# A decoder step on one core: other orders at the stage boundaries

## The reference

```python
x += W_out [ dilated sliding-window attention(q,k,v) || conformer convolution(glu) ],  [q|k|v|glu] = RMSNorm(x) @ W_in
x += PEER(RMSNorm(x));   y = RMSNorm_final(x)

# PEER: 8 heads, 128 x 128 product keys, top 16 of the candidates, 16384 experts
q = x @ w_query                      # per head two halves of 128
s1, s2 = q1 @ k1.T, q2 @ k2.T        # top 16 of each, sums, top 16 of the sums -> eid, softmax -> gate
act = gelu(sum(exp_u[eid] * x))      # one dot product per chosen expert
out = sum(gate * act * exp_v[eid])
```

## Time and profile before

| | |
|---|---|
| median of three runs | 1831.47 us |
| the profiled execution | 1835.39 us, of which span 1833.6 us |
| TensorE busy | 1738.1 us (95%) |
| VectorE busy | 1430.8 us (78%) |
| ScalarE busy | 620.0 us (34%) |
| GpSimd busy | 442.8 us (24%) |
| chain that ended last | TensorE 60%, VectorE 16%, ScalarE 3%, DMA 2% |
| granted TensorE clock, mean | 0.982 of full speed |
| moved by DMA | 397 MB, 216 GB/s |

### The profile page before, as it was taken

One profiled execution on the slowest core, in us unless ns is written; L12 is line 12 of the kernel. 1 busy time (PEld: TensorE's weight loads), 2 busy tenths in 40 slices (PEclk: granted clock), 3 DMA queues, 4 the chain that ended last, 5 costly groups with the idle time before them and its releaser, 6 DMA issues.

```text
span 1833.6 us, 26115 instructions
## 1 busy us (share of the span) xinstructions
PE 1738.1 (95%) x9365; PEld 1523.3 (83%) x9365; DVE 1430.8 (78%) x3029; ACT 620.0 (34%) x1022; POOL 442.8 (24%) x510
## 2 busy tenths in 40 slices
PE   7998889899999899979999999999999999989986
PEld 6777664477676478879999999999999999988885
DVE  5887552279999788857888888887888888878887
ACT  5223451211111177643333333333333333322322
POOL 1000000013232200023444444433333333332210
PEclk9999999899999999989999999999999999999998
DMA  8314603222211257688889889888888889877763
GB/s 264 112 65 169 248 1 110 96 70 70 80 47 57 70 157 218 210 286 291 290 306 325 296 308 332 296 299 299 289 309 317 305 308 318 313 256 265 259 217 132
DMA packets 200148, 396.97 MB, mean 216 GB/s; under 512 B 14863, under 2 KB 132653, under 8 KB 198605
## 3 DMA queue, kind: packets, MB, share of 16 engines
q1 hardware_dynamic: 158549, 244.29, 39.2%
q0 software_dynamic: 41472, 151.01, 23.4%
HBM read 359.55 MB, written 34.29 MB: 215 GB/s over the span
## 4 chain that ended last, share of the span: by engine, by line
PE 60%; DVE 16%; issue 3%; ACT 3%; DMA 2%; POOL 0%; SPq 0%; DVEq 0%; ACTq 0%
PE bank L1496 23%; PE bank L1436 23%; PE bank L1470 5%; PE bank L1418 4%; PE bank L1357 3%; PE bank L1395 2%; DVE ef L1900 1%; DVE catT_then_yT L2054 1%; DVE y L2075 1%; DVE sc L1825 1%; DVE i L1822 1%; DVE i L1831 1%; DVE y0s L2075 1%; ACT u_high L1636 1%; DVE bits L1863 1%
## 5 line engine op out<-in xcount | busy, mean ns | idle before, releaser
L1496 PE MATMUL bank<-p_high,v_high 128*128 128x400 f32 x880 | 304.1, 346 | 7.5 <-DVE v_low L2000 7.5
L1496 PE MATMUL bank<-p_high,v_low 128*128 128x400 f32 x880 | 305.1, 347 | 0.0
L1496 PE MATMUL bank<-p_low,v_high 128*128 128x400 f32 x880 | 304.8, 346 | 0.0
L1436 PE MATMUL bank<-h_high,u_high 128*128 128x400 f32 x768 | 264.3, 344 | 10.6 <-DVE u_low L2000 9.9
L1436 PE MATMUL bank<-h_high,u_low 128*128 128x400 f32 x768 | 266.7, 347 | 0.0
L1436 PE MATMUL bank<-h_low,u_high 128*128 128x400 f32 x768 | 264.9, 346 | 0.0
L1735 POOL DMA_INDIRECT rows<-in_u_rows,row_u x144 | 194.2, 1349 | 279.4 <-DVE dots L2066 242.7
L1735 POOL DMA_INDIRECT rows<-in_v,row_u x144 | 162.6, 1129 | 351.5 <-DVE y L2075 283.6
L1642 ACT CAST p_high<-gel 128x400 fp32r<-128x400 f32 x128 | 67.4, 527 | 375.3 <-DVE gel L2045 373.7
L2000 DVE TENSOR_TENSOR v_low<-vv,v_high 128x1024 fp32r<-128x1024 f32 x110 | 134.7, 1225 | 65.6 <-ACT v_high L1636 65.5
L1418 PE MATMUL bank<-h2T,early 128*128 128x400 f32 x512 | 179.2, 505 | 5.5 <-ACT gel L1583 5.5
(11 more groups left out here) (254 smaller groups left out, 2962.3 us busy)
## 6 DMA issues: line engine op xcount, KB each, us to landing
vv<-in_v SPq DMA_DIRECT2D x110, 512.0 KB, 7.2
u<-in_uT SPq DMA_DIRECT2D x96, 512.0 KB, 4.8
gates_kept<-staged SPq DMA_DIRECT2D x10, 2560.0 KB, 10.0
gate<-gates_kept SPq DMA_DIRECT2D x30, 800.0 KB, 7.4
early<-in_uT SPq DMA_DIRECT2D x32, 512.0 KB, 3.4
w_in_sb<-in_w_in SPq DMA_DIRECT2D x9, 1024.0 KB, 8.1
u<-in_v SPq DMA_DIRECT2D x18, 512.0 KB, 6.4
wq<-in_w_q SPq DMA_DIRECT2D x16, 512.0 KB, 3.5
```

Of the source, the lines that this page charges most:

```text
L1436: ins = pe.matmul(a_ps[par][:, 0:DT], x[:, par, k], y, start=(z == 0), stop=(z == len(order) - 1))
L1496: ins = pe.matmul(out, x[:, c, at:at + P], y, start=(opens and c == 0 and n == 0), stop=(closes and c == CG - 1 and n == 2))
```

## The change

It has nine edits, all of order, apart from the halved squares.
1. The first query product (head 0, half 0, z 0) is made ahead of the turn of tile 4; it waits for the first three tiles of h2T and for `joined`.
2. Eleven early activations behind head 7 in place of ten (`IN_HEADS`), so two behind the slots and eight among the gates; seven gelus ahead of the exponential.
3. The eight casts of h_high move into blocks 1 to 8 of the gates; `hot` of batch 0 is cast ahead of the last gelu.
4. In group 23 the last chunk of u is multiplied at the end of the group.
5. In groups 24 to 31 the steps m and p come as m m p p, and the piece that the group needs in product 4 comes first.
6. SyncE loads piece 2 ahead of piece 1 in group 24, and waits for one product of u fewer for it.
7. x_back and gf are loaded ahead of the transfers of group 31.
8. The product with `joins` stands behind product 2 instead of 3.
9. Squares at the end by halves, each half as soon as it is summed, the root with the first half as its bias; the sums, scales and gains in another order.

```diff
-IN_HEADS = {0: 1, 1: 2, 2: 2, 3: 2, 4: 2, 5: 2, 6: 2, 7: 10}
+IN_HEADS = {0: 1, 1: 2, 2: 2, 3: 2, 4: 2, 5: 2, 6: 2, 7: 11}
...
+    if last:
+        heavy.append(heavy.pop(heavy.index(("a", CG - 1))))
     if wide:
         heavy = [("w", x[1] + 1) if x[0] == "w" else x for x in heavy]
+        products = [(x, c) for c in range(0, CG, 2) for x in "mmpp"]
+        wanted = [x for x in heavy if x[0] not in "mp"]
+        heavy = wanted[:1] + [(x, c + n % 2) for n, (x, c) in enumerate(products[:4])] + wanted[1:4] + [
+            (x, c + n % 2) for n, (x, c) in enumerate(products[4:])] + wanted[4:]
         if not entered:
-            heavy.insert([x[0] for x in heavy].index("w"), ("w", 1))
+            heavy = heavy[1:5] + [("w", 1)] + heavy[:1] + heavy[5:]
...
                 if wide(part, gg) and m >= 2:
-                    sp.wait_ge(a_done, NK)
+                    sp.wait_ge(a_done, NK - 3 + m)
...
             def group(part, gg):
+                if (part, gg) == (PARTS - 1, GROUPS - 1):
+                    load_back()
...
-                    if what == "w":
+                    if what == "w" and GROUPS * part + gg == WIDE + 1 and at[0] in (1, 2):
+                        load_v(*of_group(part, gg, 3 - at[0]))
+                    elif what == "w":
                         load_v(*of_group(part, gg, *at))
...
                     out_projection(i)
+                if i == TILES:
+                    pe.wait_ge(h_taken, 2 * (HT // P + 1))
+                    pe.wait_ge(joined, 1)
+                    query(0, 0, 0)
                 if i:
                     turn(i - 1)
...
-                    if q == EARLY - IN_GATES - 1:
+                    if q == EARLY - IN_GATES - 2:
                         turn_slots()
...
-                if m == 3:
+                if m == 2:
                     pe.wait_ge(row_used, 2 * FETCHED)
...
-                for q in early_after(n)[:6]:
+                for q in early_after(n)[:7]:
                     gelu(q)
...
-            for k in range(KT):
-                nc.scalar.copy(h_high[:, k], h2T[:, k, P:END]).then_inc(h_rounded, 1)
...
+            for q in early_after(PH - 1)[7:-1]:
+                gelu(q)
             whole(0)
+            gelu(EARLY - IN_GATES - 1)
             for b in range(NB):
+                if 0 < b <= KT:
+                    nc.scalar.copy(h_high[:, b - 1], h2T[:, b - 1, P:END]).then_inc(h_rounded, 1)
...
+                nc.scalar.activation(out, back[0:r, i, at], ACT.Square, scale=D ** -0.5,
+                                     accum_out=(ss2 if n else ss)[0:r, i:i + 1]).then_inc(end_squared, 1)
...
+                nc.scalar.activation(rt[0:r, i:i + 1], ss2[0:r, i:i + 1], ACT.Sqrt, bias=ss[0:r, i:i + 1]
+                                     ).then_inc(end_rooted, 1)
```

More of the change, by code:

```diff
@@ L94 @@
 GEL_AT = TOP - RING * DT * 4
-assert 0 < IN_GATES < NB and RING % (CG * GROUPS) == 0
+assert 0 < IN_GATES < NB and KT < NB and RING % (CG * GROUPS) == 0
 ROW_BUFS = 4
@@ L1069, in route @@
         rt = sb("rt2", [P, TILES])
+        ss2 = sb("ss_end", [P, TILES])
         wq = sb("wq", [P, 4, KT, P])
@@ L1371, in turn, with query @@
                     ins.then_inc(x_turned, 1)
+            def query(n, half, z):
+                b, q = 2 * (n % 2) + half, 4 * (n // 2) + 2 * (n % 2) + half
+                pe.wait_ge(wq_in[b], 16 * (n // 2 + 1))
+                wait(pe, q_taken, 2 * q + z - 3)
+                for k in range(KT):
+                    ins = pe.matmul(banks[2 * half + z][:, 0:HT], wq[:, b, k], h2T[:, k, z * HT:(z + 1) * HT],
+                                    start=(k == 0), stop=(k == KT - 1))
+                if z == 1:
+                    ins.then_inc(q_done, 1)
+                else:
+                    ins.then_inc(first_half_done, 1)
             pe.wait_ge(wo_in, 16)
@@ L1386, in head @@
             def head(n):
-                it, hh = n // 2, n % 2
+                hh = n % 2
                 for half in range(2):
-                    b = 2 * hh + half
-                    pe.wait_ge(wq_in[b], 16 * (it + 1))
                     for z in range(2):
-                        q = 4 * it + b
-                        wait(pe, q_taken, 2 * q + z - 3)
-                        for k in range(KT):
-                            ins = pe.matmul(banks[2 * half + z][:, 0:HT], wq[:, b, k], h2T[:, k, z * HT:(z + 1) * HT],
-                                            start=(k == 0), stop=(k == KT - 1))
-                        if z == 1:
-                            ins.then_inc(q_done, 1)
-                        else:
-                            ins.then_inc(first_half_done, 1)
+                        if (n, half, z) != (0, 0, 0):
+                            query(n, half, z)
                 pe.wait_ge(q_taken, 4 * (n + 1))
@@ L1592, in _ @@
             nc.scalar.activation(tops[0:NS, 4], tops[0:NS, 4], ACT.Exp).then_inc(gate_exp, 1)
-            for q in early_after(PH - 1)[6:]:
-                gelu(q)
-            for k in range(KT):
-                nc.scalar.copy(h_high[:, k], h2T[:, k, P:END]).then_inc(h_rounded, 1)
             def whole(n):
@@ L2153, in _ @@
                     add_back(2, 0)
-            for i, n in SUMS_AT_END[6:10]:
-                add_back(i, n)
+            add_back(3, 0)
             scale(1)
+            scale(2)
+            add_back(1, 1)
+            scale(3)
+            add_back(2, 1)
+            add_back(3, 1)
+            gain(1)
             add_back(4, 0)
-            gain(1)
-            scale(2)
+            gain(2)
             add_back(4, 1)
-            gain(2)
-            for i in (3, 4):
-                scale(i)
-                gain(i)
+            scale(4)
+            gain(3)
+            gain(4)
 class Names(dict):
```

50 lines of the change are left out of this document (24 added, 26 removed).

## The result

| | before | changed |
|---|---|---|
| median | 1831.99 us (1830.88 to 1835.28, 4 runs beside the changed kernel) | 1799.32 us (1798.93 to 1799.66, 4 runs) |
| ratio, 95% interval | | 0.9819 (0.9802 to 0.9836) |
| span of the profiled execution | 1833.6 us | 1797.9 us |
| TensorE busy | 1738.1 us | 1728.4 us |
| mean granted clock | 0.982 | 0.988 |

The kernel is 32.7 us faster. The forecast was 51.1 us and 1780.4 us; 1799.3 lies 2.3 us above the range (1772 to 1797). The direction was right, and a third of the forecast gain isn't there.

A forecast was written before the change was run, and what follows sets the result against it. TensorE alone was taken to bound the long middle, VectorE to pace groups 24 to 31. Terms 8.1 + 12.0 + 3.3 + 22.5 + 5.7 - 0.5 = 51.1 us, off 1831.5, gave 1780.4 us; range 1772 to 1797.

The forecast's parts named there:

- the early stage to the gates: Start of the gates: TensorE's stalls on gelu and hot go, so the gates begin 7.2 us earlier.
- the 2.0 us of new wait ahead of product 6 of group 23: Group 23: with the last chunk of u moved back, product 6 waits 2.0 us for its piece to be split.
- TensorE as the bound of the paired groups at 17.4 us: Groups 24 to 31: pairing removes VectorE's waits, so TensorE narrowly binds, at 17.4 us a group for 20.3.
- the first rival: Groups 25 to 31: loads bind, 1801 us, or 1790 half-way; chance 0.17 together.
- the end: Last stage: waits for gf go, the join moves up and squares are halved; 5.7 us gained.
- the squares: End of the kernel: squares by halves save 1.5 of 14.3 us, an estimate.
- The step on the profiled execution: Whole kernel: gains read from the profiled execution, 3.9 us over the median, are durations and carry over to the median.
- the price of x_back and gf ahead of piece 2: Group 31: 2.7 MB issued ahead of piece 2 of group 30 costs 0.5 us, or 1.5 if nothing overtakes.
- The casts of h_high (0.44 us each) lie in ScalarE's slack of the blocks.: Gate blocks: the moved casts, 0.44 us each, fit in time ScalarE has to spare.
- Half clock behind product 2 of group 24: Group 24: about 3.4 us at half clock behind the 5.86 us wait, counted among the 22.5 us gained.
- the clock at routing's begin: Start of routing: shorter gaps keep TensorE's clock up in first head, spreads and turn; 4.4 us gained.
- the second rival: Two early boundaries: the clock falls all the same, 4.4 + 1.6 + 1.2 us less gain, 1788 us; chance 0.09.

The follow-up runs named there:

- experiment 4: Changed kernel with the paired steps and the order of pieces in groups 24 to 31 undone: 1808.7 us, ratio 0.9873.
- experiment 11: Changed kernel with x_back and gf issued by ScalarE on its own queue, same bytes, nearly the same time: 1797.2 us, ratio 0.9810.
- Experiment 3: Changed kernel with ScalarE's casts of h_high and u_high moved from the beginning to the middle of the gate blocks: 1794.3 us, ratio 0.9794.
- experiment 8: Changed kernel with x_back and gf in four portions in groups 28 to 31, and casts of h_high and u_high in mid-block: 1788.6 us, ratio 0.9763.
- experiment 2: Changed kernel with x_back and gf loaded in four portions, one behind the load of W in each of groups 28 to 31: 1793.2 us, ratio 0.9788.
- experiment 5: Changed kernel with the first query product back behind the turn of the last tile: 1804.9 us, ratio 0.9852.

## Why the forecast was 18 us too fast

**Right.** The bound in the middle, the early stage to the gates (7.2 us, to a tenth), the 2.0 us of new wait ahead of product 6 of group 23 (1.85), TensorE as the bound of the paired groups at 17.4 us (17.5), no binding load in groups 25 to 30 (the first rival; seven of the experiments show one or two single waits of 0.2 to 1.8 us there, not one in each group), the end (5.3 for 5.7), the squares (1.2 for 1.5). The step on the profiled execution, that the gains carry over to the median, isn't the fault either: the ratio gives 33.2 us, and the terms as the runs have them (6.7 or more, 7.3 - 0.5, 4.3, 11.6 from experiment 4, 5.3) give 34.7 or more.

**The failed step, 6 to 7 us: the price of x_back and gf ahead of piece 2.** I wrote: "If not, piece 2 lands 4.5 us into group 31 instead of 2, and product 6 waits 1.5 us. I take 0.5." The order was seen, and the sum was made from positions instead of bytes. The rows had the number: 293 GB/s at a DMA share of 0.85 is 345 GB/s when all is busy, and 2.7 MB at that rate are 7.8 us. Even that is short of the 10.2 that experiment 11 works out, since the gathers take their part, but it is enough to see the wait. The piece landed 9.7 us into the group instead of 4.5. Group 31 took 23.9 us in place of 17.5, 6.4 us lost where the sum had 0.5. I had its slack (7.7 us for a landing in place of 6.4) and did not set the bytes against it. The rule on rings of the Trainium skill (DMA: Bandwidth & Descriptors, Queues, rings and completion order), which I cited beside it, isn't contradicted, but experiment 11 shows that the order within one ring isn't needed for the delay: it is as long from another queue.

**The second failed step, 4.4 to 5.3 us: "The casts of h_high (0.44 us each) lie in ScalarE's slack of the blocks."** ScalarE has the slack, but in the middle of a block, while TensorE is at the activation; the casts were put at its beginning, ahead of `hot`, where VectorE and TensorE are waiting. Experiment 3 moved them to the slack and had 4.4 us back. I also left u_high (1.04 us) out of the last blocks, though it stood in the code at the same place.

**Smaller.** Half clock behind product 2 of group 24 (6.8 us long, so 3.4 us of time) I counted as gone. A stretch of 3.4 us came back, in eight of the eleven kernels behind the wait ahead of product 6 of group 23, in two behind product 2 of group 24, so the chunk is worth 4.3 and not 6.7. Of the clock at routing's begin (whose parts, 2.3, 1.9 and 0.4, make 4.6 and not 4.4) 1.8 us stayed lost: the second rival, half right, in one place of the two. Its sentence that a short gap leaves the clock up held for the spreads directly behind (1.98 us), not 2 us later.

**What varies by itself.** The stage from the gates to the first product with v took 38.0 us before and 33.3 to 35.1 in eleven kernels with the change, but 37.3 in experiment 8, whose code is the same there. TensorE waits for a chunk of u in it, 2.1 to 2.8 us in the eleven and 4.5 in experiment 8, where the chunk landed 6.4 us after its issue (4.6 in experiment 2); and the kernels with 33.3 have 3.4 us less at half clock. The routing stage of these kernels, apart from experiment 5, takes 86.3 us where the out-projection starts with 5.2 us at half clock, and 85.4 where it has 3.4. Why a load or the clock falls so in one run and otherwise in the next stays open. Together with the waits of groups 23 and 24 these make the spread of the runs, some 3 us to either side, and 2.9 us of the gain in the table may be chance.

## What to carry to other kernels

A transfer that is moved forward has a price in bytes: divide its size by what the DMA engines move when all are busy (rate over share in the nearest stretch), less what other queues take of it, and compare that with the slack of the next piece that is issued *behind* it; another queue didn't help here, issuing it in portions or behind the piece did. "In the engine's slack" is a statement on a place, not on a share: look in the timeline at which point of the block the engine waits for nobody who is waited for. And an order that puts the late piece first is only as fast as that piece's load is steady: nearly the same disturbance (10.1 us to land) cost nothing in the old order and 6.6 us in the new (13.9 us).

## What the runs showed of the hardware

The DMA engines of the core moved 363 GB/s at a share of 1.03 over 18.5 us with the queues of SyncE and GpSimd filled, and 355 at 0.99 with ScalarE's as well. One 512 KB piece landed 3.7 us after its issue with nothing large ahead of it, 13.9 us after it with 2.7 MB ahead in its queue, and 15.7 with them in another. With the same 2.7 MB issued 0.5 us behind it a piece took 4.2 us.

The granted clock was at its lower level from 358.5 to 361.9 us (0.51), although the rows of TensorE from 350 us on have gaps of only 0.69, 0.33 and 0.38 us, and it fell 2.5 us after the last of them. In experiment 2 it fell at 355.8, 1.6 us after the same gap, while the spreads ran (2.25 us for 1.98). At the gates' end gaps of 0.48, 0.48, 1.62 and 0.48 us, one every 2.5 to 3.7 us, left the clock up (1.00 from 750 to 778 us).
